# Two transformer blocks in fp32: the second block's mixing reordered, and its branch and output products taken from the raw weights

## The reference

```
h = rms_norm(x, norm1_g) * (1 + scale1) + shift1
z = h @ w_in                          # 1024 x 4608: q, k, v, conv, gates
o = diff_attention(rope(q), rope(k), v, lam)   # 4 heads, each softmax - lam * softmax
o = rms_norm(o, subln_g, eps=1e-5) * (1 - lambda_init)
y_attn = o @ w_attn_o                 # 512 x 1024
ga, gb = split(z[conv])
u = causal_depthwise_conv(ga * sigmoid(gb), w, b)   # 31 taps, 512 channels
u = silu(layer_norm(u, conv_ln_g, conv_ln_b))
y_conv = u @ w_conv_o                 # 512 x 1024
mixed = (g_attn * y_attn + g_conv * y_conv) @ w_out # 1024 x 1024
x = x + (1 + gate1) * mixed
x = x + (1 + gate2) * ffn(rms_norm(x, norm2_g) * (1 + scale2) + shift2)
```

## Time and profile before

| | us |
|---|---|
| median of three runs | 1191.74 |
| lowest and highest | 1189.06, 1193.57 |
| the profiled execution | 1192.61 |
| its span | 1190.8 |
| TensorE busy | 1126.4 |
| VectorE busy | 844.1 |
| ScalarE busy | 547.7 |

### The profile page before, as it was taken

One profiled execution on the slowest core, in us unless ns is written; L12 is line 12 of the kernel. 1 busy time (PEld: TensorE's weight loads), 2 busy tenths in 40 slices (PEclk: granted clock), 3 DMA queues, 4 the chain that ended last, 5 costly groups with the idle time before them and its releaser, 6 DMA issues.

```text
span 1190.8 us, 20043 instructions
## 1 busy us (share of the span) xinstructions
PE 1126.4 (95%) x8620; PEld 1066.4 (90%) x8620; DVE 844.1 (71%) x1131; ACT 547.7 (46%) x605; POOL 12.1 (1%) x26
## 2 busy tenths in 40 slices
PE   5999889999999997989999999999798999999998
PEld 4877688999999896879999999999588899999998
DVE  4955567767664689986688888767989677566452
ACT  3544445565333542575554443354246745444332
POOL 4000000000000000000000000000000000000000
PEclk8999889999999998999999999999989999999998
DMA  6544233787985243434679989946334364766550
GB/s 205 177 133 132 90 125 122 283 302 259 326 299 194 97 152 107 141 107 143 228 247 317 318 291 327 327 136 208 111 107 142 107 206 158 239 221 206 185 167 36
DMA packets 127272, 228.64 MB, mean 192 GB/s; under 512 B 5797, under 2 KB 51219, under 8 KB 127185
## 3 DMA queue, kind: packets, MB, share of 16 engines
q1 hardware_dynamic: 126180, 227.11, 56.5%
q0 software_dynamic: 672, 0.06, 0.1%
q10 hardware_dynamic: 333, 0.21, 0.1%
HBM read 226.30 MB, written 1.05 MB: 191 GB/s over the span
## 4 chain that ended last, share of the span: by engine, by line
PE 67%; DVE 23%; ACT 5%; issue 4%; DMA 1%; SPq 0%; DVEq 0%; ACTq 0%
PE mm L407 58%; DVE cacc L1094 7%; DVE lo L1013 6%; ACT hi L728 3%; PE pv L450 2%; PE pa L464 2%; PE mm L432 1%; DVE ada_acc L1034 1%; DVE hf L1075 1%; DVE qk L1118 1%; DVE hf L1116 1%; DVE qk L1117 1%; DVE hf L1299 1%; PE pv L496 1%; DMA xin<-in_x_dram 1%
## 5 line engine op out<-in xcount | busy, mean ns | idle before, releaser
L1013 DVE TENSOR_TENSOR lo<-raw,hi 128x2048 fp32r<-128x2048 f32 x168 | 380.1, 2266 | 182.7 <-ACT hi L728 179.7
L407 PE MATMUL mm<-act_hi,hi 128*128 128x256 f32 x1760 | 501.0, 285 | 7.1 <-DVE act_lo L1061 5.1
L407 PE MATMUL mm<-act_hi,lo 128*128 128x256 f32 x1760 | 495.3, 281 | 0.0
L407 PE MATMUL mm<-act_lo,hi 128*128 128x256 f32 x1760 | 494.6, 281 | 0.0
L728 ACT ACTIVATE hi<-raw 128x2048 fp32r<-128x2048 f32 x168 | 316.8, 1890 | 203.4 <-PE mm L407 181.2
L407 PEld LDWEIGHTS mm<-act_hi,hi 128*128 128x128 f32 x1760 | 335.0, 190 | 13.5 <-issue 12.2
L407 PEld LDWEIGHTS mm<-act_lo,hi 128*128 128x128 f32 x1760 | 335.0, 190 | 1.0 <-issue 0.7
L407 PEld LDWEIGHTS mm<-act_hi,lo 128*128 128x128 f32 x1760 | 334.5, 190 | 0.0
L407 PE MATMUL mm<-u_hi,hi 128*128 128x256 f32 x608 | 170.6, 281 | 0.0
L407 PE MATMUL mm<-u_hi,lo 128*128 128x256 f32 x608 | 170.4, 280 | 0.0
L407 PE MATMUL mm<-u_lo,hi 128*128 128x256 f32 x608 | 169.2, 278 | 0.0
(11 more groups left out here) (246 smaller groups left out, 1097.3 us busy)
## 6 DMA issues: line engine op xcount, KB each, us to landing
raw<-in_w_in_dram SPq DMA_DIRECT2D x48, 1024.0 KB, 5.1
ada_raw<-in_ada_w_dram SPq DMA_DIRECT2D x96, 512.0 KB, 5.8
raw<-in_w_ffn_in_dram SPq DMA_DIRECT2D x88, 512.0 KB, 5.7
raw<-in_w_ffn_out_dram SPq DMA_DIRECT2D x20, 1024.0 KB, 6.0
raw<-in_w_up_dram SPq DMA_DIRECT2D x16, 1024.0 KB, 6.4
raw<-in_w_down_dram SPq DMA_DIRECT2D x16, 1024.0 KB, 6.8
raw<-in_w_out_dram SPq DMA_DIRECT2D x12, 1024.0 KB, 5.1
raw<-in_w_conv_o_dram SPq DMA_DIRECT2D x4, 1024.0 KB, 5.1
```

Source lines behind the costliest of these rows:

```text
L407: ins = pe.matmul(o, w[:, kk, fs], a[:, k, :], start=(k == 0 and i == 0 and f % 2 == 0), stop=(ends and i == 2), skip_group_check=True)
L1013: v(dve.tensor_tensor(lo[:, c % RING, 0:nk, :], raw[:, c % RING, 0:nk, :], hi[:, c % RING, 0:nk, :].bitcast(F32), ALU.subtract), "lo_done")
```

## The change

- In the second block the chunks of `attn`, `conv` and `out` are no longer split (`whole[c]`): TensorE multiplies the fp32 activations (`on`, `csq`, `gates`) by `raw` itself, one fp32 product where three fp32r ones stood. The next load into such a slot then waits for `mm_done`. The splits of these eight chunks in a layer, and those of their activations, are gone. The factor 0.5 of the gates moves into `gate1`.
- The columns of groups 3 and 4 are dealt anew, so that each holds half of `ga` and half of `gb`, and the convolution works on channels 0 to 255 first.
- In a unit VectorE now does `lo` of chunk c+2 first, then half of the unit's taps (`TAPS_IN_UNIT`: 8, in units 6 and 7 14), then the reciprocal of the sums (and in odd units the subtraction), the other taps, and `softmax_max(i+1)` last. The first softmax of a pair is scaled by ScalarE.
- The head's output is taken out of PSUM by ScalarE, into two buffers (`oB`).
- The `attn` product comes ahead of `conv`, head by head (`heads_out`), and the convolution's means stand between its parts.

```diff
-TAPS_BEFORE, ROPE_AT, TAPS_AFTER = (13, 13, 9, 12, 7, 12), ("", "", "q", "", "k", ""), (0, 0, 2, 0, 2, 0)
-TAPS_PER_UNIT = 9
-CONV_END = 5
+TAPS_AT_IN = (5, 8, 8, 8, 8, 0, 8, 0)
+TAPS_IN_UNIT = (8, 8, 8, 8, 8, 8, 14, 14)
...
+            whole[c] = len(name) == 3 and name[1] in ("attn", "conv", "out")
...
-                    sp.wait_ge(sem("lo_done"), c - RING + 1)
+                    if whole[c - RING]:
+                        sp.wait_ge(sem("mm_done"), c - RING + 1)
+                    else:
+                        sp.wait_ge(sem("lo_done"), int(splits[c - RING]))
...
+                if len(acts) == 1:
+                    return ((raw[:, slot], acts[0]),)
+                a_hi, a_lo = acts
+                return (hi[:, slot], a_hi), (hi[:, slot], a_lo), (lo[:, slot], a_hi)
...
+                heads_out(0, (0, 1))
+                apply_v(ptB, v2, (ATTN_HEADS - 1) * P, P, 0, True)
...
+                mean_of(cacc, 2)
+                heads_out(0, (2,))
+                head_squares()
+                heads_out(1, (0,))
...
+                mean_of(csq, "a")
+                heads_out(1, (1, 2))
+                heads_out(0, (3,))
+                heads_out(1, (3,))
+                for half in range(2):
+                    chunk((l, "conv", half), 0, csq, ready=None if half else "uc_ready")
...
-                        chunk((l, "out", half), j, act_hi, act_lo, ready=None if half else "mixed_split", per=2)
+                        chunk((l, "out", half), j, gates, ready=None if half else "mixed_ready", per=2)
...
+                for i in range(UNITS):
+                    name, j = todoB(l)[i]
+                    advance(groups[name][1][j])
+                    count = TAPS_IN_UNIT[i]
+                    taps(count // 2)
+                    probs2(i)
+                    taps(count - count // 2)
                     if i + 1 < UNITS:
                         softmax_max(i + 1, sB)
...
+                    if i % 2 == 0 and i >= 4:
+                        head_normed(i // 2 - 2)
```

More of the change, by code:

```diff
@@ L213, in two_blocks @@
         landed.append(count[c % RING])
+    whole = [False] * NCH
+    for name, (_, ids) in groups.items():
+        for c in ids:
+            whole[c] = len(name) == 3 and name[1] in ("attn", "conv", "out")
+    splits = list(np.cumsum([not w for w in whole]))
     with ExitStack() as ctx:
@@ L720, in split @@
             def split(c):
-                if c >= NCH:
+                if c >= NCH or whole[c]:
                     return
@@ L949, in _ @@
                         log_tables()
-                    if i % 2 == 1 and i >= 3:
-                        high(hf[:, h % 2, :], o_hi[:, h, :], "on_ready", "o_hi_ready")
+                head_of(ATTN_HEADS - 1)
+                wait("centred")
+                a(act.activation(csq[:, :, :], cacc[:, :, :], ACT.Square), "csq_ready")
+                rstd_from(P, 1, (ATTN_HEADS - 1) % 2)
+                rstd_from(GF, 1, 0)
+                for k in range(GT):
+                    wait("ln_ready")
+                    a(act.activation(csq[:, k, :], cacc[:, k, :], other(ACT.Silu), bias=pcols(("lnb", l))[:, k:k + 1]), "uc_ready")
                 for half in range(2):
-                    steps((l, "attn", half))
-                    for pair in (2 * half, 2 * half + 1):
-                        k = slice(2 * pair, 2 * pair + 2)
-                        high(gates[:, k, :], act_hi[:, k, :], "mixed_ready", "mixed_hi_ready", scale=0.5)
+                    steps((l, "conv", half))
                 for c in out_chunks(l):
@@ L1007, in split @@
             def split(c):
-                if c >= NCH:
+                if c >= NCH or whole[c]:
                     return
-                dve.wait_ge(sem("hi_done"), c + 1)
+                dve.wait_ge(sem("hi_done"), int(splits[c]))
                 nk = chunks[c][0]
@@ L1428, in _ @@
+                head_normed(3)
+                wait("rstd_ready")
+                for k in range(GT):
+                    v(dve.scalar_tensor_tensor(out=cacc[:, k, :], in0=cacc[:, k, :], scalar=pcols(("lng", l))[:, k:k + 1], in1=rstd[:, 0, :],
+                                               op0=ALU.mult, op1=ALU.mult), "ln_ready")
                 for half in range(2):
-                    steps((l, "attn", half))
                     gate_branch("attn", half)
-                    pairs = [slice(2 * pair, 2 * pair + 2) for pair in (2 * half, 2 * half + 1)]
@@ L1432, in _ @@
-                    for k in pairs:
+                for half in range(2):
+                    steps((l, "conv", half))
+                    gate_branch("conv", half)
+                    for pair in (2 * half, 2 * half + 1):
+                        k = slice(2 * pair, 2 * pair + 2)
                         v(dve.tensor_tensor(gates[:, k, :], gates[:, k, :], gates[:, 8 + k.start:8 + k.stop, :], ALU.add), "mixed_ready")
-                    for k in pairs:
-                        low(gates[:, k, :], act_hi[:, k, :], act_lo[:, k, :], "mixed_hi_ready", "mixed_split", scale=0.5)
+                    v.settle()
```

267 lines of the change are left out of this document (122 added, 145 removed).

## The result

| | before | after |
|---|---|---|
| median, us | 1192.24 | 1231.44 |
| lowest and highest | 1189.06, 1193.57 | 1229.97, 1233.51 |
| the profiled execution | 1192.61 | 1229.97 |
| its span | 1190.8 | 1228.1 |
| TensorE, VectorE, ScalarE busy | 1126.4, 844.1, 547.7 | 1145.6, 789.0, 517.1 |

The changed kernel is slower by 3.25%: ratio 1.0325, 95% interval 1.0307 to 1.0344, of four runs each. The forecast was 1242, range 1221 to 1262. VectorE and ScalarE have 55 and 31 us less to do, and the span grew by 37.3 us.

A forecast was written before the change was run, and what follows sets the result against it. TensorE, busy for 95% of the span, was taken as the bound. Mixings of +20.0 and +17.3 and ends of 2 x 6.1 gave 49.5; 1192.6 + 49.5 = 1242 us, range 1221 to 1262.

The forecast's parts named there:

- The start: Ahead of the first scores: TensorE's 7 us wait goes, and layer 0's first softmax is done at 458.7.
- The units: Layer 0, first softmax to unit 5's probabilities: 65.4 us, ending at 524.1, +10.3 us against before.
- twelve terms: Alternating VectorE and ScalarE pieces from the first softmax to unit 5's probabilities, summing to 65.4 us.
- The rival without turn-taking: In the units ScalarE's `hi` comes early enough that TensorE sets the pace: 1184 to 1193 us; chance 0.07.
- turn-taking: In the units `lo` needs `hi`, behind `exps`, which needs the softmax: a steady pair takes 25.2 us, before 16.6.
- ScalarE's tables: Table loads in the units cost 1.28 us each; five at the skill's 2.66 would lose 6.9 more a layer.
- fp32: Raw products of `attn`, `conv`, `out`: 0.433 us each against 0.353 for three fp32r, +10.3 us a layer.
- The rival of a cheap fp32: Raw fp32 products on TensorE cost only as much as three fp32r, 0.353 us: 1221 us; chance 0.04.
- Behind the units: Unit 5's probabilities to the mixing's end: 67.4 work, 10.3 fp32, 0.7 fourth head, 1.5 clock; 79.9 us in all.
- The end: After the mixing's last product: a late transfer's split delays x's update, +4.6 us a layer, and 1.5 for the clock.
- The low-clock rival: TensorE stays at 1.2 GHz through the units, costing 11 us a layer: 1264 us; chance 0.10.

The follow-up runs named there:

- e1_order: The changed kernel with VectorE's unit reordered: division and next softmax first, then `lo` and all taps; 1190.63 us, ratio 0.999.
- e13_softmax_last: The changed kernel with VectorE's `lo` moved behind the division and all taps, the softmax still last; 1197.7 us, ratio 1.0021.
- e2_copy: The changed kernel with the gates evacuated by ScalarE's copy instead of tanh, leaving out table loads; 1228.8 us, ratio 1.0307.
- e3_order_copy: The changed kernel with both the unit order of e1_order and the gates evacuated by copy instead of tanh; 1190.92 us, ratio 0.9996.
- e5_tail: The changed kernel with the second feed-forward chunk's split moved behind x's update on VectorE and ScalarE; 1223.03 us, ratio 1.024.
- e9_order_outsplit: The changed kernel with the unit order of e1_order and `out` split again, only `attn` and `conv` raw; 1170.76 us, ratio 0.9806.
- e6_warm: The changed kernel with 11 small fp32 products on TensorE ahead of the probabilities' wait in units 1, 3 and 5; 1231.92 us, ratio 1.0319.
- e4_three: The changed kernel with three fp32r products on old buffer contents in place of each raw fp32 product; 1219.94 us, ratio 1.0235.

## Why the prediction was right, and where its sizes were off

**The start.** The wait ahead of the first scores went, and `exps(0)` came 62.06 us after the layer's start; the forecast had 62.2. Right.

**The units.** The forecast had 65.4 us from `exps(0)` to the transposes of unit 5; it took 63.9. VectorE's pieces were 6.1 to 6.2 in even units (6.3 forecast) and 7.1 in odd ones (7.3). The stretches from a softmax to the next `lo` were 2.9, 2.9, 5.6, 3.4, 7.9 and 3.4 against 3.0, 3.0, 5.7, 3.65, 7.9 and 3.65; in the last, 2.8 are idle and VectorE norms a head in the rest. So no single term is off: most of the twelve terms are too long by 0.1 or 0.2, in sum by 0.7 in VectorE's pieces and by 0.7 in ScalarE's. The mechanism is shown by more than the reading: `e1_order` takes it away with the same instructions, `e13_softmax_last` weakens it by the amount counted ahead, and a relief of ScalarE shortens the units only where turns are taken (`e2_copy` against `e3_order_copy`). The rival without turn-taking failed in its premise: VectorE's work in a pair is indeed under TensorE's, but work that has to be done in turns is not hidden by its sum being small.

**ScalarE's tables.** In the rows above the activation behind a load starts 0.02 us after the load's 1.28, and the load itself 0.01 after the instruction before it. The forecast's sum went by this. In `e2_copy`, with two loads fewer between `exps(4)` and the next `hi`, the units get 2.8 us shorter, 1.4 a load: its own 1.28, and about 0.1 by which two activations in a row overlap. The 2.66 us a switch of the Trainium skill ("ScalarE: Activation LUTs", What ACT_TABLE_LOAD costs) do not agree with the trace here. The forecast counted five loads in the turn-taking, but its own sum up to unit 5 holds three (one after unit 1, two after unit 3); with three, the figure of the skill would have given an estimate of 1250, not 1256.

**fp32.** The 128 records of `out` take 27.79 us, (27.79 - 0.38) / 127 = 0.216 apart, the figure from the 16 records of before. The rival of a cheap fp32 is excluded by that row. The four passes of the Trainium skill ("FP8 and Floating Point Precision", TensorE Precision Notes) against three would be 0.47 for a product, an estimate; the row has 0.432, so the trace does not bear out the ratio. That the overhead of each instruction makes the difference, as the forecast had it, is not shown.

**Behind the units.** 79.9 forecast, 77.4 and 77.9 measured; this is the step that was most off, by up to 2.5 us a layer. 1.5 of it was for the clock. It was wrong as a difference: the earlier trace rows showed a loss after a long wait, but the kernel before had lost about as much in this stretch already, in layer 0 after its own wait of 1.78:

```profile
510.00:515.00 5.00, 3.22 (x20) 0.85 0.66 210
515.00:520.00 5.00, 5.00 (x36) 0.80 0.34 111
...
```

From the transposes to the next scores it took 8.04 us there, 7.95 in the changed kernel, and 6.50 in layer 1 of before at full clock. That layer lost its 1.6 us a little later, at the mean of the squares (3.22 us, 1.64 in layer 0). So both kernels pay about 1.5 us a layer, the changed one 1.9 in layer 1, and the difference is 0 to 0.3, not 1.5.

The second term that was off is fp32 itself. The products of `conv`, `attn` and `out` took 46.4 us before, waits left out (11.8, 11.9 and 22.8, rounded), and 55.4 after (13.8, 13.8 and 27.8), in both layers: +9.0, not +10.3. The price of a tile was right for `out`, where they follow without a break; `conv` and `attn` had before taken 23.7 for 64 tiles, 1.1 more than the 22.6 of the pace in the earlier trace rows. On the other side stands a wait for the fourth head of 1.3, where 0.7 was counted. With these three terms the stretch of layer 0 is accounted for within 0.3 us.

**The end.** +6.1 a layer forecast, +5.2 and +5.3 measured. VectorE and ScalarE there, in the changed kernel:

```profile
598.69 2.29 DVE L1054 TENSOR_TENSOR lo<-raw,hi 128x2048 fp32r<-128x2048 f32 x1 [4.70 <-ACT hi L768]
600.90 3.94 DVE L1368 SCALAR_TENSOR_TENSOR x<-mm,cols,x 128x256 f32<-128x256 f32 x8
```

```profile
596.75 1.91 ACT L768 ACTIVATE hi<-raw 128x2048 fp32r<-128x2048 f32 x1 [5.15 <-DMA raw<-in_w_ffn_in_dram]
```

It is the chain of the forecast: transfer, `hi`, `lo`, and x's update behind it. `lo` ends 2.6 us after the last product, not 3.2. Of the 5.2, 4.0 are the longer wait; the other 1.2 are the sum of squares itself, slowed (5.28 and 5.38 for its 16 records, 4.10 before), with a granted clock of 0.75 in 600 to 605. The forecast had 4.6 and 1.5 for the two. `e5_tail` and `e9_order_outsplit` take the wait away in two ways.

**The low-clock rival** (1264). The clock did fall, to 0.50, in more stretches than before, but in the units it was back at 0.99 or 1.00 within 7 us of each restart, and with it held higher in `e6_warm` they take as long. Its price behind the units, 1.5 and 1.9, is one that the kernel before pays too.

**Together.** The forecast was 12.2 us of span too high: 7.9 in the two mixings (the rounds too long by 1.5 each, the stretches behind them by 2.5 and 2.0, the starts by 0.2), 1.7 at the ends, and 2.7 where no difference was forecast, ahead of the first mixing and in the feed-forward. Of those 2.7 no edit is the cause that I can name.

**What the change is made of.** By the runs and traces: turn-taking some 20 us a layer, fp32 9.0, the late transfer 5 to 6.5. Against this the new mixing gains: with the order put back, `e1_order` reaches unit 5's transposes of layer 0 104.9 us after the layer's start, where before it was 117.3. In layer 1 it is 104.6 against 119.9. Nearly all of it lies ahead of the units: `exps(0)` comes 62.1 to 62.4 us after the start, not 75.2, and the units behind it take 42.5 against 42.1 and 44.7. Which of the edits to the first groups brings how much of it was not tried by itself. These 12.4 and 15.3 us pay for most of fp32 and the end; the stretch to the feed-forward is 195.7 and 196.7 against 194.9 and 197.6. With `out` split, 9 to 11 us a layer are left of it as a gain.

## What to carry to other kernels

Where two engines run in order and feed each other twice in a loop, look at what stands between the last instruction that hands over and the first that needs the other: the loop is hidden only if that stretch is as long as the other's answer, however little both are busy. The order within a unit was worth 20 us a layer here, and with it right the splits saved on `out` were still a loss of 10. And when a copy is removed, count how long its source is now held: a slot that was free after the split is now free after the product, and the next stage's first transfer starts that much later.

## What was not expected of the hardware

A low clock in the page's row is not yet a loss, and not yet harmless either; it depends on who sets the pace there. In `e6_warm` the granted clock around unit 1's transposes rose from 0.54 to 1.00 and the units took the same 63.9 us. Behind unit 5, where TensorE is the bound, the same 48 products and what stands with them took 6.5 us at full clock and 7.9 to 9.4 where it had fallen. Neither its fall nor its return is the same each time: in the kernel before, after nearly the same wait (1.78 and 1.83 us), it fell in layer 0 and stayed at 1.00 in layer 1. And in `e4_three` and in the changed kernel TensorE waits 7.5 us there and then runs the same instructions up to the next scores, and yet layer 0 of `e4_three` had 0.83 at 525 to 530, where the changed kernel had 1.00. Why is left open.
